# A fused gated-delta / Conformer / FFN layer: who evacuates the first eight down sums, and where the eighth plain block's relu and scaling stand

## The reference

```
hf = rmsnorm(x, g_pre_ffn) @ w_up          # 1024 -> 4096
f  = square(relu(hf))
y  = x + rmsnorm(f @ w_down, g_post_ffn)   # 4096 -> 1024
```

## Time and profile before

| | |
|---|---|
| median of 3 runs | 1079.61 us (1078.01 to 1079.72) |
| profiled execution, time / span | 1079.36 us / 1077.6 us |
| PE busy | 1053.3 us, 98% |
| DVE / ACT / POOL busy | 746.1 / 567.1 / 631.8 us |
| mean granted clock of TensorE | 0.995 |
| first down job starts | 721.34 us |
| first up pair starts | 753.82 us |

### The profile page before, as it was taken

How to read it: one execution, slowest core, us unless ns; L and a number is a source line. 1 busy time by engine, 2 the same in 40 slices (tenths; PEclk the granted TensorE clock), 3 DMA queues, 4 the chain that set the end, 5 groups by cost and what they waited for, 6 DMA issues and landing times.

```text
span 1077.6 us, 22149 instructions
## 1 busy us (share of the span) xinstructions
PE 1053.3 (98%) x8135; PEld 1032.6 (96%) x8135; DVE 746.1 (69%) x1246; ACT 567.1 (53%) x1037; POOL 631.8 (59%) x542
## 2 busy tenths in 40 slices
PE   8999999999999999999999999998999999999996
PEld 6999999999999999999999999998999999999996
DVE  7987997969879698796977757597445444444335
ACT  7854655455554555555646865753444444343631
POOL 1986486674965848658584443635555655545631
PEclk9999999999999999999999999999999999999998
DMA  6223122231122311223221162122233222322302
GB/s 239 98 67 110 64 59 74 80 108 63 40 91 79 108 63 39 90 81 100 71 79 59 43 244 79 40 78 80 79 97 99 81 79 83 112 78 78 115 10 82
DMA packets 32666, 92.07 MB, mean 85 GB/s; under 512 B 4704, under 2 KB 12256, under 8 KB 32608
## 3 DMA queue, kind: packets, MB, share of 16 engines
q1 hardware_dynamic: 32608, 91.29, 25.8%
HBM read 82.76 MB, written 8.52 MB: 85 GB/s over the span
## 4 chain that ended last, share of the span: by engine, by line
PE 82%; DVE 7%; POOL 4%; issue 3%; ACT 1%; DVEq 0%; POOLq 0%; ACTq 0%
PE ps L737 31%; PE ps L1146 13%; PE ps L1096 12%; PE ps L746 5%; PE ps L1178 5%; PE ps L939 1%; DVE ps L1850 1%; PE ps L992 1%; POOL o_a L2534 1%; POOL in_lo L2534 1%; PE ps L908 1%; PE ps L929 1%; DVE work L1847 1%; PE ps L1001 1%; PE ps L966 1%
## 5 line engine op out<-in xcount | busy, mean ns | idle before, releaser
L2534 POOL TENSOR_TENSOR w_lo<-raw,w_hi 128x1024 fp32r<-128x1024 f32 x100 | 242.0, 2422 | 214.9 <-ACT w_hi L1265 102.7
L737 PE MATMUL ps<-in_hi,w_hi 128*128 128x288 f32 x944 | 285.9, 303 | 0.9 <-issue 0.9
L737 PE MATMUL ps<-in_hi,w_lo 128*128 128x288 f32 x944 | 283.8, 301 | 0.0
L737 PE MATMUL ps<-in_lo,w_hi 128*128 128x288 f32 x944 | 282.1, 300 | 1.0 <-POOL in_lo L2534 1.0
L1850 DVE SCALAR_TENSOR_TENSOR ps<-work,ct,ps 128x512 f32<-128x512 f32 x240 | 180.6, 752 | 7.2 <-DVE work L2015 1.6
L737 PEld LDWEIGHTS ps<-in_hi,w_hi 128*128 128x128 f32 x944 | 177.7, 188 | 1.8 <-issue 1.3
L737 PEld LDWEIGHTS ps<-in_lo,w_hi 128*128 128x128 f32 x944 | 177.4, 188 | 1.5 <-POOL in_lo L2534 1.4
L737 PEld LDWEIGHTS ps<-in_hi,w_lo 128*128 128x128 f32 x944 | 177.6, 188 | 0.5
L1847 DVE TENSOR_TENSOR o_a<-o_a,ps 128x576 f32<-128x576 f32 (+1 forms) x64 | 43.3, 678 | 110.5 <-PE ps L1146 73.3
L2534 POOL TENSOR_TENSOR w_lo<-t_pair,w_hi 128x1024 fp32r<-128x1024 f32 x18 | 43.4, 2408 | 44.4 <-ACT w_hi L1716 31.4
L1146 PE MATMUL ps<-f_hi,w_hi 128*128 128x288 f32 x288 | 62.5, 298 | 4.9 <-DVE o_a L2357 4.9
(11 more groups left out here) (386 smaller groups left out, 2863.7 us busy)
## 6 DMA issues: line engine op xcount, KB each, us to landing
raw<-w_all_in SPq DMA_DIRECT2D x135, 512.0 KB, 3.7
work<-s_in_in SPq DMA_DIRECT2D x8, 512.0 KB, 3.3
s_sample_out<-work SPq DMA_DIRECT2D x8, 512.0 KB, 2.6
xt<-x_t_in SPq DMA_DIRECT2D x4, 576.0 KB, 6.6
xt<-x_t_in SPq DMA_DIRECT2D x2, 1152.0 KB, 7.2
y_out<-o_a SPq DMA_DIRECT2D x16, 144.0 KB, 1.7
halo<-halos_in SPq DMA_DIRECT2D x9, 156.0 KB, 3.5
conf_rows_out<-c_rows SPq DMA_DIRECT2D x8, 135.0 KB, 2.0
```

The costliest lines, as they stand in the source:

```text
L737: t = mm(dense_ps(n, j, h), a[:, w, k], b[:, k, h * HALF:(h + 1) * HALF], start=r == 0, stop=r == PASS_MM // 2 - 1)
L2534: return gp.tensor_tensor(out, a, b, op)
```

## The change

The sums of the first group's 8 down jobs are copied out of PSUM by ScalarE, with a semaphore of its own (`d_copied`), and not by VectorE. The 8 copies are placed by hand in ScalarE's queue. `plain_relu(7)` stands ahead of `plain_squares(6)` there. In VectorE's queue `plain_scale(7)` and `plain_low(6)` stand ahead of the last form's sum `x_add(0, B21, B22)`. The values of `dve_read` that others wait for are 8 lower throughout.

```diff
@@ down_half
                 if n_is(g_, 0) and i < 2:
                     pe.wait_ge(act_read, 158 + 2 * i)
+                elif n_is(g_, 0) or n_is(g_, 1) and i < 2:
+                    pe.wait_ge(d_copied, 8 * g_ + i - 1)
                 else:
-                    pe.wait_ge(dve_read, 8 * g_ + i - 1)
+                    pe.wait_ge(dve_read, 8 * (g_ - 1) + i - 1)
@@ down_job: dve_read, 48 (+ i - 3) -> dve_read, 40 (+ i - 3)
@@ ScalarE
             down_cast(landed_out(10, 1), 3, 1, [(job_done, 158)])
+            plain_relu(7)
             plain_squares(6)
-            plain_relu(7)
             plain_squares(7)
+
+            def down_copy(i):
+                act.wait_ge(job_done, UP_DONE + i + 1)
+                nc.scalar.copy(two(o_a[:, i]), job_ps(i % 2)).then_inc(d_copied, 1)
+
+            down_copy(0)
             h_cast(H_B22[0], h_of(B22))
             h_cast(H_B11[0], h_of(B11))
+            down_copy(1)
             down_cast(landed_out(10, 2), 0, 2, [(job_done, 160)])
             x_cast(4, H_E[0], sum_of(1))
             x_cast(5, H_D[0], sum_of(0))
+            down_copy(2)
             down_cast(landed_out(10, 3), 1, 3, [(in_ready, H_READY + 5)])
...
+            down_copy(3)
+            down_copy(4)
             cast_sums(0, 0, 2)
+            down_copy(5)
             cast_one(0, None)
             cast_raw(1, 2, 4)
+            down_copy(6)
             cast_differences(0, 2, 6)
+            down_copy(7)
             round_(2, 0)
@@ VectorE: down_add
-                if n_is(g_, 0):
-                    ve.tensor_copy(two(o_a[:, i]), job_ps(i % 2)).then_inc(dve_read, 1)
-                else:
-                    tt(two(o_a[:, i]), two(o_a[:, i]), job_ps(i % 2), ALU.add).then_inc(dve_read, 1)
+                tt(two(o_a[:, i]), two(o_a[:, i]), job_ps(i % 2), ALU.add).then_inc(dve_read, 1)
@@ VectorE: order
             plain_low(5)
+            plain_scale(7)
+            plain_low(6)
             dve.wait_ge(in_ready, H_READY + 3)
             x_add(0, B21, B22, ALU.add)
-            plain_scale(7)
-            plain_low(6)
             plain_low(7)
-            down_add(0, 0, 1)
             x_low(4, H_B22, h_of(B22))
             x_low(5, H_B11, h_of(B11))
-            down_add(0, 1, 2)
             x_low(6, H_E, sum_of(1))
             x_low(7, H_D, sum_of(0))
-            down_add(0, 2, 3)
             dve.wait_ge(in_ready, H_READY + 5)
             sums(0, 2, None, (landed_at(2, 0), landed_at(2, 1)))
             one(2, None)
-            down_add(0, 3, 4)
             differences(2, None)
-            for i in range(4, 8):
-                down_add(0, i, i + 1)
             round_(2, 0)
```

More of the change, by code:

```diff
@@ L522, in build @@
         u_copy, u_sum, u_out = sem("u_copy"), sem("u_sum"), sem("u_out")
+        d_copied = sem("d_copied")
         block = ctx.enter_context(nc.Block())
@@ L1170, in down_job @@
                     if i < 4:
-                        pe.wait_ge(dve_read, 48)
+                        pe.wait_ge(dve_read, 40)
                     else:
-                        pe.wait_ge(dve_read, 48 + i - 3)
+                        pe.wait_ge(dve_read, 40 + i - 3)
                 for k in ks:
@@ L1827, in _ @@
                     log_exp()
-                act.wait_ge(dve_read, 48 + i + 1)
+                act.wait_ge(dve_read, 40 + i + 1)
                 if i >= 4:
```

## The result

| | before | after |
|---|---|---|
| median of 6 runs | 1079.66 us (1078.01 to 1080.39) | 1072.73 us (1072.12 to 1073.23) |
| ratio, 95% interval | | 0.9936 (0.9924 to 0.9949) |
| profiled execution, time / span | 1079.36 / 1077.6 us | 1073.02 / 1071.0 us |
| first down job starts | 721.34 us | 721.59 us |
| first matmul of the first up pair | 753.66 us | 747.14 us |

The account below looks back on a forecast made before the run. TensorE, busy 98% of the span, was taken as the bound; removing 1.39 + 3.50 of waiting, 1.59 of low clock and 0.48 around the stops (6.96 us) gave 1072.7 us, range 1071.2 to 1075.3.

Parts of the forecast that it names:

- The prize: From the first down job to the first up pair: 32.48 us less eight undisturbed jobs of 25.52, so 6.96 us.
- Both stops: TensorE's waits at down jobs 2 and 4 for VectorE's copies, 1.39 and 3.50 us, both to go.
- 0.48 "around the two stops": Time at the waits of jobs 2 and 4 that the listed waits leave out, 0.48 us of the 6.96.
- the 1.59 of the low clock: Behind the 3.50 us wait, 18 matmuls took 3.98 us instead of 2.39 at full clock: 1.59 us more.
- The range: For the case of both waits gone (chance 0.80, at 1072.7): its own range of 1071.1 to 1073.3 us.
- The copy's price: ScalarE's copy of 128x576 from PSUM, shown in no row: taken as 0.65 us, bounds 0.62 and 0.75.
- The order as cover: VectorE's scaling ahead of the last form's sum lets ScalarE square block 7 earlier, making room for the copies.
- The smallest margin: GpSimd's split of weight 83, ready by 733.1 at the latest, wanted by job 4 at 734.10: 1.0 us.
- One stop remains at job 4: Rival: weight 83 or job 2's copy is late; 1073.7 us, or 1075.3 with the low clock; chance 0.10.
- Given back at the first up pair: Rival: weights 85 to 88 come late, up pair starts s later, gain 6.96 - s; around 1075.7, chance 0.02.
- No change: Rival: the two stops had another cause that the copies merely hid; time stays at 1079.6 us, chance 0.04.
- The queue locks TensorE out: Rival: job 5's copy behind `cast_sums` stops job 7; a loss once sums come after 747.1; chance 0.04.

Follow-up runs that it names:

- Copies alone: The changed kernel with both queues back in their old order, only the copies moved to ScalarE: 1073.21 us, ratio to before 0.9938.
- kernels with repeated copies: The changed kernel with every down copy made twice (1072.77 us), or only job 2's copy made seven times (1074.68) or eleven times (1079.50).
- the order alone: The changed kernel with the copies back on VectorE in their old places, relu and scaling still moved ahead: 1077.17 us, ratio to before 0.9976.
- the first group: Four follow-up kernels, variants of the changed kernel in order, copies or their placing, run on one chip beside the kernel before (1079.68 us).
- copy 2 seven times: The changed kernel with job 2's copy made seven times on ScalarE instead of once, stop of 2.04 us at job 4: 1074.68 us, ratio 0.9959.

## Why the prediction was right

The forecast was 1072.7 and the measurement 1072.73. By its own steps:

**The prize.** Both stops and the low clock are gone; the first matmul of the up pair comes 32.32 - 25.55 = 6.77 us earlier counted from the first down job. I had said 6.96. The step that was mis-sized is the stretch itself: I took the start of the first job on one side and the modelled end of the last job (753.82) on the other, instead of two starts. Counted from start to start the stretch before was 753.66 - 721.34 = 32.32, so 0.16 of my prize were never there. As 0.48 "around the two stops" was what the other terms left over, the error lands in it; but the term that was too large is the 1.59 of the low clock. The stop of 2.04 us above, without a low clock behind it, cost 0.22 around it, so two stops cost about 0.44; that leaves 6.77 - 4.89 - 0.44 = 1.44 for the clock. Part of the difference is the longer first pair of matmuls behind the stop (0.50 instead of 0.42), which I had counted in both terms. Such tenths can't be told in the medians, whose runs spread by a microsecond: that the median fell within 0.03 us of the forecast is luck. In the profiled execution 0.25 us of the gain are hidden by a first job that starts later than before, so the up pair starts 6.52 us earlier in the span; the span is 6.6 shorter and the profiled time 6.34, and these last differences lie outside this stage and are not explained.

**The range.** The narrow range ended at 1073.3, which doesn't follow from what was given for it (0.1 above the median of the shown runs gives 1072.8). The measured runs reach 1073.23.

**The copy's price.** Taken as 0.65, measured 0.64 (8 copies, mean 639 ns). The Trainium skill (VectorE: DVE Perf Modes, section "The TRN2 errata") gives 172 + n cycles at 1.2 GHz for ScalarE out of PSUM and 120 + n at 0.96 GHz for VectorE; worked out for 576 elements that is an estimate of 0.62 and 0.73 us. The trace agrees within 4%: 0.64 and 0.75.

**The order as cover.** I wrote that the scaling in front of the sum "is what makes room for the copies". That was too strong. Copies alone reach 1073.21, with one stop of 0.44 us. The relu's move is worth nothing that shows here. The last form's sum itself took 1.36 us, the shorter end of my 1.4 to 2.9.

**The smallest margin.** I put it at the weight 83: ready by 733.1, wanted at 734.10. The split began about as planned (729.83 against 729.6) but took 2.41 us and not my 3.17 to 3.47, so the weight was there at 732.24 and wanted at 734.35. GpSimd's timeline after, splits of 83 and 84:

```profile
729.83 2.41 POOL L2541 TENSOR_TENSOR w_lo<-raw,w_hi 128x1024 fp32r<-128x1024 f32 x1 [5.23 <-ACT w_hi L1698]
733.42 3.56 POOL L2541 TENSOR_TENSOR w_x<-raw,w_x 128x1024 fp32r<-128x1024 f32 x1 [1.18 <-ACT w_x L1698]
```

**One stop remains at job 4** (0.10): didn't happen. With the copies alone the two `h_cast` began even later than this rival supposed (728.66, in an execution whose first job began at 721.9), and job 4 still didn't stop. The split of 83 took 2.40 us and ended at 734.83; job 4 started at 728.90 + 6.38, about 735.3, which the stop at job 2 had put off by half a microsecond. With a split of 3.17 us, the least that I had reckoned with, it would have ended at 735.60, a few tenths late. So the rival's condition was met there, and its price for the split was too high. The section "HAM oscillation" of the Trainium skill (TensorE: Matmul & The Clock Gate), which I cited here, says that idleness brings the lower clock back. That work earns the full one, and that the turning point varies from run to run, stands in the same page's section "What's actually happening", and the variation is told there of the rise. For the fall only the runs here speak (last section).

**Given back at the first up pair** (0.02): no. The split of 85 ended at 742.05 against my 741.7, wanted at 747.14. **No change** (0.04): ruled out, the stops went and the time with them. **The queue locks TensorE out** (0.04): it didn't happen, and what a late copy costs is seen in the kernels with repeated copies. The sums were done at 738.06; my plan said 738.2, the point of no return was 747.1. The kernel with the copy of job 2 made eleven times comes to zero gain at a stop of 4.72 us, near the 5.1 that I had worked out as break-even for a stop with a low clock.

## What to carry to other kernels

Look first at the few waits of the bounding engine and ask what stood in front of the late instruction in its queue. VectorE was busy for only 69% of the span, and yet its 0.75 us copy behind 6.33 us of other work stopped TensorE for 3.50 us; putting the copy between two of the long instructions was worth as much as giving it to another engine. Write both queues out with times, and give each copy out of PSUM its deadline (here one job, 3.19 us). The margins found that way told in all eight experiments where a stop would be and how long, to within its range or a tenth; two of the times missed their ranges, the copies alone by 0.3 us below and the order alone by 0.2 above, the latter because the low clock behind the stop was left out.

## What the runs showed of the hardware that I had not expected

**A slow pair of VectorE and GpSimd instructions is mostly waiting inside an instruction.** The two remainders took 6.33 us before, 6.34 with the order alone and 3.88 after, for the same work. I had planned with 6.33 for the remainders and 1.21 for `sums`; they took 3.88 and 3.41, so that the sums came out on time by two errors that cancel, which is luck. VectorE's timeline after, the last form's sum first:

```profile
724.47 1.36 DVE L1863 TENSOR_TENSOR f_tmp<-xt 128x1152 f32<-128x1152 f32 x1
...
730.84 3.88 DVE L1863 TENSOR_TENSOR in_lo<-f_tmp,in_hi 128x1152 fp32r<-128x1152 f32 x2 [1.32 <-ACT in_hi L1659]
734.65 3.41 DVE L1863 TENSOR_TENSOR t_pair<-raw 128x1024 f32<-128x1024 f32 x1
737.99 0.68 DVE L1863 TENSOR_TENSOR t_one<-raw 128x512 f32<-128x512 f32 x1
```

The split of 84 ended at 733.42 + 3.56 = 736.98, and `sums` ended 1.08 behind that, about its time alone (1.21). In the other direction this split began at 733.42 and ended 2.3 us behind the remainders' end (734.72), about its own 2.4. Before, `differences` (3.43) began 0.03 behind a split and ended 1.07 behind that split's end, and the small split that followed took 2.27 where it takes 1.30 after. The last form's sum, 2.90 before, began 1.68 ahead of the end of a split (720.92 + 3.43 = 724.35) and ended 1.22 behind it; after, it began 0.13 ahead of that split's end (724.60) and took 1.36. The 6.33 come out in the same way: the remainders began inside the split of 83 and ended, at 738.56, 1.21 behind the end of the split of 84 (737.35). So each waited for the other's whole instruction and then ran at its normal pace; instructions with an input in PSUM (0.75 us) didn't stretch beside a split. The Trainium skill (SBUF — State Buffer, section "SBUF: two separate sides") states just this: VectorE instructions with two SBUF inputs and GpSimd instructions that read SBUF take a shared pair of ports for the whole instruction, whichever starts first. The rows agree. In this stage the last form's sum and the two remainders took 4.0 us less, `sums` and `differences` together as much as before (4.6); with the 6.0 of the copies this is within 0.7 us of the 9.3 by which VectorE's busy time fell. For a forecast it means: don't take a contended duration from a row; take the duration alone and add the rest of whatever GpSimd has under way.

**When the clock falls behind a stop.** Stops of 0.43, 0.44, 1.39 and 2.04 us left the full clock in the profiled executions; 2.91, 3.50 and 4.72 us were followed by a stretch near 1.2 GHz that cost 1.4 to 2.0 us, as much as a second, shorter stop. The fall need not come with the stop: behind 2.91 us four pairs of matmuls ran at the full pace, and the low level came only when TensorE had been at work again for over a microsecond. TensorE's timeline of the order alone:

```profile
737.90 0.42 PE L1149 MATMUL ps<-f_hi,w_hi 128*128 128x288 f32 x2
738.16 0.49 PE L1149 MATMUL ps<-f_hi,w_lo 128*128 128x288 f32 x2
738.45 0.68 PE L1149 MATMUL ps<-f_lo,w_hi 128*128 128x288 f32 x2
738.93 0.68 PE L1149 MATMUL ps<-f_hi,w_hi 128*128 128x288 f32 x2
```

Whether it comes goes by the run, at 2.91 us and perhaps at 2.04: of nine executions of the order alone, two took 1075.72 and 1076.09 at a mean granted clock of 0.997, the others 1077.06 to 1078.00 at 0.995 to 0.996; of five with copy 2 seven times, four took 1074.12 to 1074.93 and one 1076.30. Even the kernel before has, among the fifteen executions of the first group, one of 1077.75 at 0.997; the others are at 0.994 to 0.996. That this is the low clock coming or not coming is a reading of the sizes, the difference of about 1.5 us each time; only the profiled executions show it.
